# Three transformer blocks on one core: tokens in column order of the grid, and neighbourhood attention over 160 of 256 keys a tile

## The chip, the cores and the metric

The kernel is one program on one core of a Trainium2 chip, started once. The metric is device time in microseconds. Engines are named as in the profile: PE (matrix products, with its weight loads as PEld), DVE (vector), ACT (scalar), POOL (GpSimd), SP (the engine that issues nearly all transfers). All data are float32; "fp32r" marks operands that PE takes in one pass, and many products are made of three such passes over a high and a low part.

## The reference

256 tokens of 1024 features go through a first block of two layers and a second block.

- Layer 0: differential attention and latent attention over all 256 tokens (with rotary positions), output projection, residual times alpha, layer norm; then a mixture of experts (32 experts, two a token, grouped routing), residual times alpha, layer norm.
- Layer 1: neighbourhood attention, then the same tail with another mixture of experts.
- Second block: RMS norm, a gated linear recurrence with a causal convolution beside retention, output projection, and a gated feed-forward part with a causal convolution.

Neighbourhood attention sees the tokens as a grid of 4 rows and 64 columns, token = 64 row + column. It has 16 heads of 64. A query in column c attends to all 4 rows and to 16 columns, from clip(c - 8, 0, 48) on:

```
col_start = clip(cols - kw // 2, 0, GRID_W - kw)
s = einsum(q_row, k_win) * d**-0.5 + bias(head, row offset, column offset)
p = softmax(s over the 4 x 16 window);  o = p @ v_win
```

Layer 0 and the experts don't care in which order the tokens stand, as long as positions go with them. The second block does, since its convolutions, recurrence and retention run along the sequence.

## The kernel before

**Layout.** X holds the tokens as two tiles of 128 (partition = token in the tile). XT and MT hold features by tokens. The order is that of the sequence: tile 0 is grid rows 0 and 1, tile 1 is rows 2 and 3.

**Order of the work.** Each engine runs its own list of instructions, written out by hand; semaphores tie them together. On SP the loads stand in one queue in program order: each waits until the slot of the ring buffer that it fills is free, and everything behind waits with it. QKV weights (I_QKV), output weights (I_OO) and then the expert weights of layer 1 (load_experts) follow each other; the bias of the neighbourhood attention, one transfer of 128 x 16 x 384 numbers (source line 686 of the profile), stands behind the fourth QKV weight. It goes to G, in the arena. LNR holds the gain and bias of the coming norm; POOL loads it (norm_rows). The expert layer 0 keeps a copy of X there (XP).

**Neighbourhood attention** (functions `attention` on PE, ACT and DVE, a loop of POOL). For every head h and both query tiles t:
- PE makes the scores of 128 queries against all 256 keys (line 1037), for two heads at once since a head has 64 rows of the array, into banks 4 to 7.
- DVE adds the bias and takes the minimum in one instruction (2086); masked keys have a bias of -1e30. ACT takes the exponential with its sum (1623).
- DVE takes reciprocals (2093) and scales tile 1 (2095); POOL scales tile 0 (763).
- PE transposes the four 128 x 128 quarters (1049); ACT, for every fourth head DVE (2107), copies them out (1610).
- PE multiplies by the values, two matmuls of 256 columns a head (1062); ACT and DVE write the result as high and low part (1595, 2057).

PE works in pairs of heads: scores of pair i, transposes of pair i-2, values of pair i-3. PE's in-order list, the probability buffers PN (six) and PTN (four) set the order.

**After it.** The output projection (project_out_split, line 918) starts in the order of the pairs; POOL makes the low parts of the first two of its weight rows (767). DVE normalizes (mixed_norm), PE transposes X and makes the router's logits (1211), puts alpha times X into banks 0 to 3 with a diagonal matrix (`residual`, line 1216), and fills waits with matmuls that nobody reads (keep_clock, 1024). Banks 0 to 3 then gather the experts' outputs: for each pair of experts a matmul with the 0/1 matrix SWT (scatter, 1088; SWT is written by DVE, 2152) adds rows of outputs to their tokens. The gather (1074) uses SEL, its weighted copy is SELW. When 16 pairs are done, DVE normalizes from the banks into X.

**Loads of the expert layer.** Six weights of 2 MB a pair of experts. Ten places take them in turn; the first six of layer 1 wait for the end of QKV, for the end of attention (a_pv) or for the output projection, the rest for the pair before them in their place.

Of the kernel before, what the change touches and what calls it, by code (L numbers as in the profile page):

```python
# [15 lines left out]
P = 128  # L16
# [23 lines left out]
BIAS_ROWS = 6  # L40

# [23 lines left out]
def shape_constants():  # L65
# [3 lines left out]
    def rotation(theta, rot):  # L69
        inv = f(theta) ** (-np.arange(0, rot, 2, dtype=f) / f(rot))  # L70
        ang = np.arange(SEQ, dtype=f)[:, None] * inv[None].astype(f)
        both = np.stack([np.cos(ang), np.sin(ang)]).astype(f)
        return both.reshape(2, T, P, -1).transpose(2, 0, 1, 3).reshape(P, -1)
# [8 lines left out]
        rotation(500000.0, 2 * A_HALF),  # L82
        rotation(500000.0, B_ROPE),
# [30 lines left out]
def bass_two_blocks(nc, x, w_in, w_uq, w_ukv, w_o, w_qkv, na_bias, w_o2, ln_rows, rows, cols, w_route,  # L114
                    w_gate, w_up, w_down, w_in2, gates, w_out2, ffn_up, ffn_down, table, table2, out):
    with ExitStack() as ctx:
# [57 lines left out]

        ident, earlier = KT[:, K_ID:K_ID + P], KT[:, K_LT:K_LT + P]
# [35 lines left out]
        G = cut(4352, C_HEADS, BIAS_ROWS * GRID_W)  # L211
# [339 lines left out]
        def _(sp):  # L551
            sp.dma_start(KT[:, :], table).then_inc(x_loaded, 16)
            sp.dma_start(X[:, 0, :], x[0:P, :]).then_inc(x_loaded, 16)
            sp.dma_start(X[:, 1, :], x[P:SEQ, :]).then_inc(table2_loaded, 16)
# [113 lines left out]

            src, view = items[I_EIN[0]][0:2]
# [32 lines left out]
        def _(pool):  # L702
# [54 lines left out]
            pool.wait_ge(x_ready, 4)  # L757
            norm_rows(2)
            low_tiles(S_QKV, range(3 * TILES, 6 * TILES))
            for a in range(N_NA0, N_NA0 + C_HEADS):  # L760
                m = a % len(PN)
                pool.wait_ge(a_rec, a - N_NA0 + 1)
                nc.gpsimd.tensor_scalar(PN[m][:, 0, :], PN[m][:, 0, :], sm[:, m, 0:1], None,
                                        ALU.mult).then_inc(a_p0, 1)
            for c in range(ROWS_FIRST):
# [24 lines left out]
        def _(pe):  # L790
# [238 lines left out]
            def attention(a0, n, q, k, v, probs, probs_t, free):  # L1029

                for i in range(n // 2 + 3):
                    if i < n // 2:
                        for a in (a0 + 2 * i, a0 + 2 * i + 1):
                            if a - a0 >= 4:
                                pe.wait_ge(free, a - 3)
                            for t in range(T):
                                last = nc.tensor.matmul(bank[4 + a % 4][:, t * SEQ:(t + 1) * SEQ], q(a - a0, t), k(a - a0),
                                                        start=True, stop=True)
                            last.then_inc(a_score, 1)
                    if 0 <= i - 2 < n // 2:  # L1040
                        for a in (a0 + 2 * i - 4, a0 + 2 * i - 3):
# [5 lines left out]
                            for t in range(T):  # L1047
                                for kt in range(T):
                                    last = nc.tensor.transpose(
                                        bank[a % 2][:, kt * SEQ + t * P:kt * SEQ + (t + 1) * P],  # L1050
                                        probs[a % len(probs)][:, t, kt * P:(kt + 1) * P], ident)
                            last.then_inc(a_pt, 1)
                    if 0 <= i - 3 < n // 2:
# [6 lines left out]
                        for kt in range(T):  # L1060
                            for e in range(2):
                                last = nc.tensor.matmul(bank[2 + pair % 2][64 * e:64 * e + 64, 0:SEQ],
                                                        v(a - a0 + e, kt), probs_t[(a + e) % 4][:, kt, :],
                                                        start=(kt == 0), stop=(kt == T - 1))
# [134 lines left out]
            def moe_layer(l, name):  # L1199

                if l == 0:
                    pe.wait_ge(route_loaded, 16)
                for t in range(T):
                    if t:
                        keep_clock(6, 1)
                        transposes_by_token(name, X, x_ready, 4 * l, [t])
                        keep_clock(5, 1)
# [7 lines left out]
                    for half in range(2):  # L1215
                        nc.tensor.matmul(bank[2 * t + half][:, :], residual, X[:, t, 512 * half:512 * half + 512],
                                         start=True, stop=False, skip_group_check=True)

                keep_clock(5, 2)
# [1436 lines left out]
```

## Time and profile before

| | us |
|---|---|
| median of three timed runs (1503.03 to 1504.11) | 1503.18 |
| the profiled execution's own time | 1501.31 |
| its span, first to last instruction | 1499.4 |

| engine | busy us | share |
|---|---|---|
| PE | 1455.7 | 97% |
| DVE | 563.1 | 38% |
| ACT | 476.1 | 32% |
| POOL | 153.8 | 10% |

The stages by PE's chain: layer 0's attention to about 142 us, its experts to about 582, QKV of layer 1 from 591 to 660, neighbourhood attention from 661 to 689, projection and router to 726, experts to 1154, then the second block. Busy shares are averages over these. A time in the span is counted from its start; the timeline's rows begin with it, and the DMA share of a window is that of all 16 DMA engines. PE's clock was granted in full throughout.

### The profile page before, as it was taken

What the parts mean: (1) busy time and instruction counts of PE and PEld (TensorE: products, weight loads), DVE (VectorE), ACT (ScalarE), POOL (GpSimd) and SP (SyncE); (2) the same over time, 40 slices, a digit from 0 to 9 for tenths busy, and PEclk for the clock granted to TensorE, in tenths of its full rate; (3) what the DMA queues carried; (4) which work ended last, traced back from release to release, by engine and by line L of the source; (5) the groups of instructions that cost most, each with busy time, mean ns of one, the idle gap of its engine ahead of it and who ended that gap; (6) DMA issues with size and microseconds to landing.
All of it is one profiled execution on the core that took longest, in us unless ns stands there. A gap on an engine that the chain in (4) does not pass through costs nothing.

```text
span 1499.4 us, 19281 instructions
## 1 busy us (share of the span) xinstructions
PE 1455.7 (97%) x7750; PEld 881.1 (59%) x7750; DVE 563.1 (38%) x1161; ACT 476.1 (32%) x837; POOL 153.8 (10%) x124
## 2 busy tenths in 40 slices
PE   8989999999999998999999999999999999999997
PEld 7766444544544445977544545445444786888886
DVE  6675111121111113037311111111111488689965
ACT  4561111111111113456111111111111672687654
POOL 0211000000000002952100000000000710001200
PEclk9999999999999999999999999999999999999999
DMA  8657999999999999835999999999999946464410
GB/s 304 243 234 265 398 424 427 428 428 426 427 428 428 425 423 399 307 151 235 380 408 427 430 427 427 428 427 427 427 426 412 351 170 224 171 223 169 174 52 29
DMA packets 77669, 502.70 MB, mean 335 GB/s; under 512 B 4880, under 2 KB 6160, under 8 KB 50320
## 3 DMA queue, kind: packets, MB, share of 16 engines
q1 hardware_dynamic: 77008, 497.27, 81.4%
q0 software_dynamic: 576, 4.19, 0.7%
q8 instruction: 65, 1.06, 0.3%
q14 instruction: 20, 0.16, 0.0%
HBM read 500.40 MB, written 1.05 MB: 334 GB/s over the span
## 4 chain that ended last, share of the span: by engine, by line
PE 82%; DVE 7%; DMA 5%; ACT 2%; SPq 2%; issue 1%; POOL 0%; DVEq 0%; ACTq 0%
PE bank L1129 26%; PE bank L1170 13%; PE bank L990 9%; PE bank L1074 7%; DMA ring<-in_w_up 4%; PE bank L1456 4%; PE bank L1484 3%; PE bank L1088 3%; DVE w_low L2524 2%; SPq L649 2%; PE bank L899 2%; PE bank L1458 2%; PE bank L918 1%; PE bank L837 1%; DVE arena L2548 1%
## 5 line engine op out<-in xcount | busy, mean ns | idle before, releaser
L1129 PE MATMUL bank<-ring,arena 128*64 128x512 f32 x1280 | 280.6, 593 | 8.9 <-issue 5.5
L1129 PEld LDWEIGHTS bank<-ring,arena 128*64 128x64 f32 x1280 | 93.2, 137 | 191.3 <-issue 189.0
L1129 PE MATMUL bank<-arena 128*64 128x512 f32 x576 | 167.8, 592 | 0.0
L2143 DVE TENSOR_TENSOR arena<-arena,bank 128x512 f32<-128x512 f32 x32 | 22.0, 688 | 371.9 <-PE bank L1129 371.9
L1170 PE MATMUL bank<-ring,arena 128*64 128x512 f32 x640 | 141.7, 595 | 2.4 <-ACT arena L1638 2.4
L1456 PE MATMUL bank<-x_split,w_high 128*128 128x512 f32 (+1 forms) x408 | 136.3, 385 | 0.2 <-DVE x_split L1951 0.2
L1074 PEld LDWEIGHTS bank<-SEL,x_by_row 128*128 128x128 f32 x1024 | 116.7, 192 | 25.8 <-issue 24.3
L2157 DVE SCALAR_TENSOR_TENSOR y_low<-bank,ST,y_high 128x512 fp32r<-128x512 f32 x64 | 48.1, 751 | 202.4 <-ACT y_high L1642 202.4
L1074 PE MATMUL bank<-SEL,x_by_row 128*128 128x128 f32 x1024 | 122.8, 278 | 0.0
L1642 ACT ACTIVATE y_high<-bank,ST 128x512 fp32r<-128x512 f32 x64 | 44.0, 687 | 245.6 <-PE bank L1170 245.6
L1129 PEld LDWEIGHTS bank<-arena 128*64 128x64 f32 x576 | 54.8, 137 | 107.7 <-issue 107.7
L1458 PE MATMUL bank<-x_split,w_low 128*128 128x256 f32 (+1 forms) x408 | 111.5, 273 | 0.0
L2524 DVE TENSOR_TENSOR w_low<-ring,w_high 128x1024 fp32r<-128x1024 f32 x72 | 97.7, 1359 | 28.2 <-ACT w_high L1860 28.0
L712 POOL TENSOR_TENSOR qkv_low<-ring,qkv_high 128x1024 fp32r<-128x1024 f32 x24 | 58.2, 2441 | 457.8 <-DVE X L1997 449.8
L1635 ACT COPY arena<-bank 128x512 f32<-128x512 f32 x30 | 17.6, 586 | 253.6 <-PE bank L1074 253.6
L1170 PEld LDWEIGHTS bank<-ring,arena 128*64 128x64 f32 x640 | 45.9, 137 | 84.2 <-issue 84.2
L1456 PEld LDWEIGHTS bank<-x_split,w_high 128*128 128x128 f32 x408 | 76.3, 187 | 15.1 <-DVE x_split L1951 0.3
L1170 PE MATMUL bank<-arena 128*64 128x512 f32 x272 | 85.0, 595 | 0.0
L1129 PE MATMUL bank<-first_over_features,arena 128*64 128x512 f32 x192 | 84.4, 592 | 0.0
L1860 ACT CAST w_high<-ring 128x1024 fp32r<-128x1024 f32 x72 | 75.5, 1052 | 25.3 <-PE bank L1484 25.2
L1458 PEld LDWEIGHTS bank<-x_split,w_low 128*128 128x128 f32 x408 | 77.2, 189 | 0.0
L712 POOL TENSOR_TENSOR in_low<-ring,in_high 128x1024 fp32r<-128x1024 f32 x12 | 29.4, 2488 | 451.8 <-DVE X L1997 448.8
(369 smaller groups left out, 2222.7 us busy)
## 6 DMA issues: line engine op xcount, KB each, us to landing
ring<-in_w_gate SPq DMA_DIRECT2D x32, 2048.0 KB, 25.7
ring<-in_w_up SPq DMA_DIRECT2D x32, 2048.0 KB, 22.4
ring<-in_w_down SPq DMA_DIRECT2D x32, 2048.0 KB, 22.8
arena<-in_w_gate SPq DMA_DIRECT2D x18, 2048.0 KB, 22.5
arena<-in_w_down SPq DMA_DIRECT2D x16, 2048.0 KB, 24.1
arena<-in_w_up SPq DMA_DIRECT2D x14, 2048.0 KB, 16.5
ring<-in_ffn_up SPq DMA_DIRECT2D x12, 2048.0 KB, 7.9
ring<-in_w_in SPq DMA_DIRECT2D x8, 2048.0 KB, 15.0
```

Of the source, the lines that this page charges most:

```text
L712: nc.gpsimd.tensor_tensor(low, src, high, ALU.subtract).then_inc(w_lo, 1)
L990: last = nc.tensor.matmul(part_(bank[g % 2 * 2 + t]), a, b, start=(part_ is parts[0] and c == 0 and n == 0), stop=(part_ is parts[-1] and ...
L1074: last = nc.tensor.matmul(bank[6 + c // 4][:, c % 4 * P:(c % 4 + 1) * P], x_rows(t, c), SEL[:, t, :], start=(t == 0), stop=(t == T - 1))
L1088: last = nc.tensor.matmul(bank[2 * t + half][:, :], SWT[:, t, :], y[:, 512 * half:512 * half + 512], start=False, stop=False, skip_group_c ...
L1129: last = nc.tensor.matmul(bank[4 + m][64 * e:64 * e + 64, :], XG[:, c, 64 * e:64 * e + 64], w[e][:, c, :], start=(c == 0), stop=(c == C - 1))
L1170: last = nc.tensor.matmul(bank[6 + half][64 * e:64 * e + 64, :], HT[:, j, 64 * e:64 * e + 64], down_rows(e, j)[:, 512 * half:512 * half + ...
L1456: nc.tensor.matmul(bank[f % 4][:, :].rearrange("p (a b) -> p a b", a=2)[:, :, a:b], WHI[f % WBUF][:, c, :], XSPLIT[:, :, c, a:b], start=(a ...
L1458: last = nc.tensor.matmul(bank[f % 4][:, a:b], WLO[f % WBUF][:, c, :], XHI[:, c, a:b], start=False, stop=(b == SEQ and c == C - 1), skip_g ...
L1484: last = nc.tensor.matmul(bank[4 + 2 * t + half][:, :], a, w.rearrange("p a b -> p (a b)"), start=(c == 0 and n == 0), stop=(c == DOWN_T - ...
L1860: nc.scalar.copy(WHI[k % WBUF][:, :, :], src).then_inc(w_hi, 1)
L2157: v.scalar_tensor_tensor(YLO[:, cols_], bank[6 + half][:, :], slot_gate, YHI[:, cols_].bitcast(F32), ALU.mult, ALU.subtract).then_inc(s["y ...
L2524: v.tensor_tensor(WLO[k % WBUF][:, :, :], ffn_weights(k)[1], WHI[k % WBUF][:, :, :], ALU.subtract)\
```

## The change

1. x is loaded in column order: token = 4 column + row. Tile 0 is grid columns 0 to 31, tile 1 is 32 to 63. The rotary tables of layer 0 are laid out alike.
2. A query tile needs 40 columns, that is 160 keys: tile 0 keys 0 to 159, tile 1 keys 96 to 255. Scores, bias, exponential, scaling and copy work on 160 keys or queries. The gap of PN between the two parts is cleared by POOL.
3. The transposes become two whole ones, one of 64 rows and one of 32 rows a head. The values become three matmuls of 160, 96 and 64 columns.
4. The bias comes in 16 transfers (2 tiles, 2 sets of heads, 4 grid rows of the query), of 32 partitions each and pieces of 232 numbers. Its layout in DRAM is unchanged, so DVE reads it with the grid row as innermost index, 64 numbers apart. Heads 13 to 15 lie in LNR, so the load waits for the end of layer 0's last norm (x_ready 4), and norm_rows(2) moves behind the last bias reduction.
5. In layer 1 the residual and the scatter put rows back into sequence order: the diagonal matrix becomes four permuted ones (TO_ROWS, in SEL and SELW, written by POOL), eight matmuls instead of four, in the place of layer 1's keep_clock; SWT of layer 1 is written with permuted columns.

```diff
+KEYS = (GRID_W // 2 + NA_COLS // 2) * GRID_R          # 160
+KEYS_FROM = (0, SEQ - KEYS)                           # 0, 96
...
-            sp.dma_start(X[:, 0, :], x[0:P, :]).then_inc(x_loaded, 16)
-            sp.dma_start(X[:, 1, :], x[P:SEQ, :]).then_inc(table2_loaded, 16)
+            by_column = x.rearrange("(r c) d -> c r d", r=GRID_R)
+            for t, loaded in enumerate((x_loaded, table2_loaded)):
+                sp.dma_start(X[:, t, :], by_column[GRID_W // T * t:GRID_W // T * (t + 1)]).then_inc(loaded, 16)
...
+        def bias_of(h, t):
+            buffer, at = bias_block(h, t)
+            whole = buffer[:, at:at + GRID_R * GRID_W].rearrange("p (r j) -> p r j", j=GRID_W)
+            return whole[:, :, 0:KEYS // GRID_R].rearrange("p r j -> p j r")
...
+            def load_bias():
+                sp.wait_ge(x_ready, 4)
+                for t in range(T):
+                    for heads in (range(IN_ARENA), range(IN_ARENA, C_HEADS)):
+                        for r in range(GRID_R):
+                            begin = (2 - r // 2 * 2) * GRID_W + KEYS_FROM[t] // GRID_R
+                            first = r % 2 * GRID_W + GRID_W // T * t
+                            sp.dma_start(bias_blocks(t, heads)[r:P:GRID_R],
+                                         na_bias[first:first + GRID_W // T, heads[0]:heads[-1] + 1, begin:begin + BIAS_W])\
+                                .then_inc(bias_loaded, 16)
...
                 if i == I_QKV[3]:
-                    sp.dma_start(G[:, :, :], na_bias).then_inc(bias_loaded, 16)
+                    load_bias()
...  POOL
-            pool.wait_ge(x_ready, 4)
-            norm_rows(2)
             low_tiles(S_QKV, range(3 * TILES, 6 * TILES))
+            (two memsets and four copies: TO_ROWS; six memsets: the gap of each PN, the last two after pj_done 2 * G_OO)
             for a in range(N_NA0, N_NA0 + C_HEADS):
-                nc.gpsimd.tensor_scalar(PN[m][:, 0, :], PN[m][:, 0, :], sm[:, m, 0:1], None, ALU.mult)
+                nc.gpsimd.tensor_scalar(PN[m][:, 0, 0:KEYS], PN[m][:, 0, 0:KEYS], sm[:, m, 0:1], None, ALU.mult)
+            pool.wait_ge(a_nb, B_HEADS + C_HEADS)
+            norm_rows(2)
...  PE, attention
+                    edge, half = KEYS - P, P // 2
+                    return [(to[:, 0:P], p[:, 0, 0:P], ident),
+                            (to[:, SEQ + edge - half:SEQ + edge], p[half:P, 0, P:SEQ], ident[half:P, half:P]),
+                            (to[:, P:KEYS], p[0:edge, 1, 0:P], ident[0:edge, 0:edge]),
+                            (to[:, SEQ + edge:SEQ + KEYS], p[:, 1, P:SEQ], ident)]
...
+                        pieces = [(0, 0, SEQ, 0), (1, 0, SEQ, 0)] if not near else \
+                            [(0, 0, KEYS, 0), (1, KEYS, SEQ, KEYS_FROM[1]), (1, KEYS_FROM[1], KEYS, KEYS_FROM[1])]
...  PE, router of layer 1
-                    for half in range(2):
-                        nc.tensor.matmul(bank[2 * t + half][:, :], residual, X[:, t, 512 * half:512 * half + 512], ...)
-                keep_clock(5, 2)
+                nc.tensor.matmul(bank[2 * to + half][:, :], residual if same else TO_ROWS[t][:, to, :],
+                                 X[:, t, 512 * half:512 * half + 512], start=(same or t == 0), ...)
...  DVE, experts of layer 1
+                    v.tensor_scalar(SWT[:, :, :].rearrange("p t (r c) -> p (t r) c", c=GRID_W),
+                                    chosen.rearrange("p (c r) -> p r c", r=GRID_R), 0.0, None, ALU.is_gt)
```

## Rows read from the trace of the kernel before

**Rows 1.** Chain that ended last (start us, us, what), end of layer 1's experts.

```profile
1119.04 30.86 DMA ring<-in_w_up
```

**Rows 2.** Windows (stretch, length, busy us and instructions of each engine, PE clock, DMA share, GB/s).

```profile
640.00:660.00 20.00, 19.92 (x124) 17.68 (x122) 0.74 (x2) 6.17 (x7) 10.72 (x5) 1.00 0.00 0
...
700.00:706.00 6.00, 6.00 (x28) 4.97 (x27) 4.51 (x7) 0.30 (x1) 0.00 (x0) 1.00 0.20 85
...
850.00:900.00 50.00, 50.00 (x268) 23.72 (x266) 9.07 (x20) 8.86 (x12) 0.00 (x0) 1.00 1.01 427
```

**Rows 3.** Windows over the attention stage (PE, PEld, DVE, ACT, POOL in this order).

```profile
667.00:683.00 16.00, 15.98 (x124) 10.33 (x121) 14.37 (x70) 15.74 (x55) 11.47 (x11) 1.00 0.90 384
683.00:690.00 7.00, 6.10 (x44) 3.68 (x43) 4.11 (x13) 6.00 (x19) 5.69 (x6) 1.00 0.00 0
```

**Rows 4.** Timeline of PE (start us, us, engine line op, tile, shape, count).

```profile
660.79 3.91 PE L1037 MATMUL bank<-arena 64*128 64x256 f32 x24 [0.87 <-DVE arena L1962]
...
667.27 1.14 PE L1037 MATMUL bank<-arena 64*128 64x256 f32 x8
...
673.70 1.14 PE L1037 MATMUL bank<-arena 64*128 64x256 f32 x8
674.77 1.09 PE L1049 MATMUL bank<-KT,arena 128*128 128x128 f32 x8
675.79 1.08 PE L1062 MATMUL bank<-arena 128*64 128x256 f32 x8
676.80 1.14 PE L1037 MATMUL bank<-arena 64*128 64x256 f32 x8
```

**Rows 5.** The same timeline in narrow windows: rows begin at single records.

```profile
674.23 0.60 PE L1037 MATMUL bank<-arena 64*128 64x256 f32 x4
...
674.45 0.39 PE L1037 MATMUL bank<-arena 64*128 64x256 f32 x2
...
674.93 0.49 PE L1049 MATMUL bank<-KT,arena 128*128 128x128 f32 x3
...
675.04 0.49 PE L1049 MATMUL bank<-KT,arena 128*128 128x128 f32 x3
```

**Rows 6.** Timeline of PE, a narrow window in the router of layer 1.

```profile
719.63 0.61 PE L1211 MATMUL bank<-WR,XT 128*128 128x36 f32 x4
```

**Rows 7.** Groups by shape: shape, count, busy us, mean ns of one.

```profile
L1610 ACT COPY arena<-bank 128x512 f32<-128x512 f32 x12 | 7.0, 581 | 0.6 <-PE bank L1049 0.5
...
L1595 ACT CAST mixed_high<-bank 128x256 fp32r<-128x256 f32 x8 | 3.0, 380 | 0.7 <-PE bank L1062 0.7
...
L2107 DVE COPY arena<-bank 128x512 f32<-128x512 f32 x4 | 2.7, 686 | 1.5 <-PE bank L1049 1.5
...
L2071 DVE COPY MT<-bank 128x256 f32<-128x256 f32 x4 | 1.7, 423 | 2.1 <-PE bank L1062 2.1
```

**Rows 8.** Timelines of POOL, DVE and PE: filling and emptying of the stage.

```profile
664.39 2.23 POOL L763 TENSOR_SCALAR arena<-arena,ST 128x256 f32<-128x256 f32 x2 [11.75 <-DVE ST L2093]
...
687.32 0.69 DVE L2107 COPY arena<-bank 128x512 f32<-128x512 f32 x1 [1.53 <-PE bank L1049]
...
689.50 0.50 PE L918 MATMUL bank<-out_high,mixed_high 128*128 128x512 f32 x1
```

**Rows 9.** Timelines of SP, DVE, POOL and ACT in the QKV stage.

```profile
585.61 5.88 SPq L686 DMA_DIRECT2D arena<-in_na_bias  x1
...
590.41 1.28 DVE L1997 SCALAR_TENSOR_TENSOR X<-X,ST,arena 128x1024 f32<-128x1024 f32 x1
...
596.34 0.37 SPq L560 DMA_DIRECT2D ring<-in_w_qkv  x1
...
618.03 0.60 POOL L704 DMA_DIRECT2D LNR<-in_ln_rows  x1
...
628.95 1.05 ACT L1679 CAST qkv_high<-ring 128x1024 fp32r<-128x1024 f32 x1 [1.83 <-PE bank L990]
```

**Rows 10.** A window while QKV weights come in pieces of 2 KB.

```profile
585.00:590.00 5.00, 3.18 (x15) 1.80 (x14) 3.63 (x6) 3.98 (x6) 4.11 (x2) 1.00 1.05 384
```

More of the change, by code:

```diff
@@ L72, in rotation @@
         both = np.stack([np.cos(ang), np.sin(ang)]).astype(f)
+        if by_column:
+            both = both.reshape(2, GRID_R, GRID_W, -1).transpose(0, 2, 1, 3)
         return both.reshape(2, T, P, -1).transpose(2, 0, 1, 3).reshape(P, -1)
@@ L1027, in x_tile, with attention, transposes_of @@
                 return XT[:, c, t * P:(t + 1) * P]
-            def attention(a0, n, q, k, v, probs, probs_t, free):
+            def attention(a0, n, q, k, v, probs, probs_t, free, near=False):
+                def transposes_of(a):
+                    p, to = probs[a % len(probs)], bank[a % 2]
+                    if not near:
+                        return [(to[:, kt * SEQ + t * P:kt * SEQ + (t + 1) * P], p[:, t, kt * P:(kt + 1) * P], ident)
+                                for t in range(T) for kt in range(T)]
+                    edge, half = KEYS - P, P // 2
[3 more added lines that the diff above has]
+                            (to[:, SEQ + edge:SEQ + KEYS], p[:, 1, P:SEQ], ident)]
                 for i in range(n // 2 + 3):
@@ L1046, in attention @@
                                 pe.wait_ge(*probs_copied(a - 2))
[L1047 to L1051, printed above, removed]
+                            for to, p, one in transposes_of(a):
+                                last = nc.tensor.transpose(to, p, one)
                             last.then_inc(a_pt, 1)
@@ L1059, in attention @@
                             pe.wait_ge(a_o, pair - 1)
-                        for kt in range(T):
+                        pieces = [(0, 0, SEQ, 0), (1, 0, SEQ, 0)] if not near else \
+                            [(0, 0, KEYS, 0), (1, KEYS, SEQ, KEYS_FROM[1]), (1, KEYS_FROM[1], KEYS, KEYS_FROM[1])]
+                        for n_, (kt, begin, end, base) in enumerate(pieces):
                             for e in range(2):
-                                last = nc.tensor.matmul(bank[2 + pair % 2][64 * e:64 * e + 64, 0:SEQ],
-                                                        v(a - a0 + e, kt), probs_t[(a + e) % 4][:, kt, :],
-                                                        start=(kt == 0), stop=(kt == T - 1))
+                                last = nc.tensor.matmul(bank[2 + pair % 2][64 * e:64 * e + 64, begin:end],
+                                                        v(a - a0 + e, kt),
+                                                        probs_t[(a + e) % 4][:, kt, begin - base:end - base],
+                                                        start=(n_ == 0), stop=(n_ == len(pieces) - 1))
                         last.then_inc(a_pv, 1)
@@ L1202, in moe_layer, with residual_rows @@
                     pe.wait_ge(route_loaded, 16)
+                def residual_rows(t, to, half):
+                    same = l == 0
+                    nc.tensor.matmul(bank[2 * to + half][:, :], residual if same else TO_ROWS[t][:, to, :],
+                                     X[:, t, 512 * half:512 * half + 512],
+                                     start=(same or t == 0), stop=False, skip_group_check=True)
                 for t in range(T):
                     if t:
-                        keep_clock(6, 1)
+                        if l == 0:
+                            keep_clock(6, 1)
+                        else:
+                            residual_rows(0, 1, 0)
                         transposes_by_token(name, X, x_ready, 4 * l, [t])
-                        keep_clock(5, 1)
+                        if l == 0:
+                            keep_clock(5, 1)
+                        else:
+                            residual_rows(0, 1, 1)
                     for copied in (tr_act, tr_dve):
@@ L1214, in moe_layer @@
                         last.then_inc(logits_done, 1)
-                    for half in range(2):
-                        nc.tensor.matmul(bank[2 * t + half][:, :], residual, X[:, t, 512 * half:512 * half + 512],
-                                         start=True, stop=False, skip_group_check=True)
-                keep_clock(5, 2)
+                    for to in ([t] if l == 0 or t == 0 else range(T)):
+                        for half in range(2):
+                            residual_rows(t, to, half)
+                if l == 0:
+                    keep_clock(5, 2)
                 pe.wait_ge(r_one, l + 1)
@@ L2125, in first_tokens, with experts @@
                 v.tensor_copy(XG[:, 4:8, :], bank[7][:, :].rearrange("p (a b) -> p a b", b=P)).then_inc(s["xg_hi"], 1)
-            def experts(s, pair, n, g, next_pair=True):
+            def experts(l, s, pair, n, g, next_pair=True):
                 dve.wait_ge(s["sel_ready"], g + 1)
@@ L2233, in moe_layer @@
                         with dve.Fori(0, PAIRS) as p:
-                            experts(s, p, r * PAIRS + p, r * (PAIRS + 1) + p)
+                            experts(l, s, p, r * PAIRS + p, r * (PAIRS + 1) + p)
                     dve.wait_ge(over_free[l], ROUNDS_MORE * PAIRS + 1)
```

77 lines of the change are left out of this document (57 added, 20 removed).

## The prediction, made before the changed kernel had run

> **What bounds the kernel now.** I read the page first, then the chain of waits, then the one stage that the change rebuilds. The page says TensorE (PE) 97% busy, with the DMA engines full through both expert layers. The chain [rows 1] and the windows [rows 2] say where each holds: the neighbourhood attention and what follows it run at PE's pace, the expert layer runs at PE's pace until its last pairs, and there PE waits 30.9 us for a weight transfer [rows 1]. In that layer the transfers run at 427 GB/s without a gap [rows 2], so its end is fixed by when its stream of transfers gets going. That start hangs on PE's progress: the DMA engines have nothing to move from 683 to 689.6 and little from 700 to 706 [rows 2, 3], because the next loads wait for the end of attention and of the output projection. So whatever the attention stage gains or loses should arrive at the end one for one, and work that is moved inside the QKV stage should cost nothing as long as PE stays gapless there.
>
> The stage lasts from 660.79 (first scores) to 689.50 (output projection), 28.7 us [rows 4, 8]. Between 667 and 683 PE is busy 15.98 of 16 us, ACT 15.74, DVE 14.37, POOL 11.47 [rows 3]. The timeline of PE [rows 4] shows one period of two heads: scores 1.07, transposes 1.02, values 1.02, sum 3.11 us, and nothing between them. PE is the bound, ACT close behind (share of 16 us times 3.11: ACT 3.06, DVE 2.79, POOL 2.23 a period).
>
> **Inside PE's period.** Narrow windows of the same timeline [rows 5] show single starts. Score records run two at a time (heads on different row halves) and start 0.22 apart: 256 columns in two passes. Four such starts are 0.86; the phase takes 1.07, so 0.21 is not columns. Eight transposes start 0.11 apart: 0.87 of 1.02, 0.15 over. Value records, again two at a time and 256 columns, are 4 x 0.216 = 0.86 of 1.02, 0.15 over. These 0.15 to 0.21 come each time that the tile shape changes (64*128, 128*128, 128*64). Four router matmuls of only 36 columns take 0.61 together with an end of 0.28, so they start 0.11 apart [rows 6], and a record with a 128-column weight does not go below 0.11, however little it streams.
>
> The Trainium skill has this as a rule (TensorEngine Tiling (Array Packing), Key Properties): changing the tiling mode drains TensorE, changing only the tile does not. The trace agrees with the first half, with the 0.15 to 0.21 above. It speaks against this change, because the new transposes of one head go through 128, 64, 32 and 128 rows.
>
> **The change part by part.** Per period of two heads:
> - Scores: 160 of 256 columns, 0.216 x 160/256 = 0.135 a start, above the 0.11 floor. 4 x 0.135 + 0.21 = 0.75, was 1.07. Bounds 0.75 and 1.07.
> - Transposes: still four a head, two whole ones (128 rows), one of 64 rows, one of 32. In order that is T1, half, edge, T4, then the same again; T4 and the next T1 share a shape. Seven phases instead of one: 7 x 0.15 = 1.05, four whole transposes 4 x 0.11 = 0.44, four small ones between 0.03 (their 64 or 32 columns at the whole one's rate, less than the floor) and 0.11, say 0.07: 0.28. Sum 1.77, was 1.02. No row shows such a small transpose. Below: no drain at all, 0.44 + 0.12 + 0.15 = 0.71. Above: each small one like a score phase, 0.11 + 0.21 = 0.32, so 4 x 0.32 + 0.44 + 3 x 0.15 = 2.17, plus 0.45 if each needs two records (2.62). I take 1.77, nearest to the rows of transposes.
> - Values: 512 columns a head become 160 + 96 + 64 = 320, in six starts instead of four: 0.86 x 320/512 = 0.54, + 0.15 = 0.69. If the 0.11 floor held for 64-column weights too: 2 x 0.135 + 4 x 0.11 + 0.15 = 0.86. I take 0.70.
> - PE's period: 0.75 + 1.77 + 0.70 = 3.22, was 3.11. PE gets 0.11 slower while the others get faster.
> - ACT: from 512 to 256 columns a copy saves 0.20 [rows 7], 0.8 ns a column. Four exponentials of 96 columns less 0.31, one and a half copies of 192 less 0.23: 3.06 to about 2.5. DVE: 1.03 ns a column by its two copies; four bias reductions 0.40, copy 0.10, multiply up to 0.10: 2.79 to 2.2. POOL: 1.1 a head [rows 8] becomes between 0.68 (in proportion) and 1.08, say 0.75. So ACT, DVE and POOL have slack, and PE alone decides.
> - The bias operand of the reduction is now read four rows at a time, 256 bytes apart; before it was contiguous. No row shows such a read by DVE. The nearest row is the contiguous copy, 1.03 ns a column: at best nothing is added, at worst (my bound) every column costs that twice, 0.16 more each; a period of DVE is then 2.9, still below PE's, so it is paid only in the filling of the pipe, six reductions, 1.0 us. I put 0.3 into the sum.
>
> The Trainium skill (SBUF — State Buffer, the note on SBUF cachelines) says that each access that crosses to a new 16-byte line pays a penalty. By it the 0.3 would be 1.0; no row here shows such a read.
>
> **What lies where.** (a) Filling, 660.79 to 667.27: the first transpose waits for scores, three heads of reductions on DVE, an exponential, and POOL's multiply. Scores give 0.32, six reductions 0.60, POOL 0.33: 1.25 earlier; the transposes of the second head waited for POOL until 666.6 [rows 8] and now come right behind the first head's, which take 0.88 instead of 0.63 inside that wait. The next scores come 1.3 earlier. (b) Five full periods, 667.3 to 683.0: 5 x 0.11 = +0.5. (c) Emptying, 683.0 to 689.50, 6.5: after it transposes and values of two pairs, (1.77 + 0.70) + 1.77, then DVE's last copy and split before the last values (from 687.2 to 688.5, with the copy of [rows 8] in it, 1.28 less 0.20), then these values 0.70: 6.02, -0.5. Sum -1.3; with the bias read -1.0.
>
> **What is moved.** Loads: the bias was one transfer issued at 585.61. It becomes 16, behind a wait for the second tile's normalization (DVE, 590.41 + 1.28 = 591.7) [rows 9]. Queued behind that wait on SP are the fifth and sixth QKV weights (the fifth issued 596.34, when its slot was freed [rows 9]) and the two output weights. One issue takes 0.37 where the queue is not full: 16 x 0.4 = 6 us, so until 598 if nothing blocks; the fifth weight comes 2 us later, and ACT first reads it at 628.95. The bytes rise from 3.1 to 3.8 MB in pieces of 928 bytes. With 2 KB pieces the engines moved 384 GB/s [rows 10]: 10 us; at half that rate 20. Attention reads it at 662, and nothing is moved from 640 to 660 [rows 2]. Cost 0. Norm rows 2: POOL's issue of 0.60 at 618.03 [rows 9] goes, and comes behind POOL's last multiply (686.5), ahead of two low rows of the output weights that PE takes from 689.5; POOL gets there over 0.3 earlier. The transfer (1 MB, 2.4 us at 427 GB/s) falls beside 4 MB of expert weights at 690 to 700 and is read at 714 or later. Cost 0, at most 0.3. POOL's new clears and copies (14 small ones, at the row of 1.08 for 256 columns at most 15 us, nearest to 4) start at 652.6, where it was idle for 11.75 us [rows 8]; the last two wait for the end of the QKV products, just before 660. Up to 11 us they are hidden.
>
> Residual: eight matmuls in place of four and four fillers of the same shape; PE's time from 706 to 726 is unchanged, and the matrices for it lie in selection buffers that are next written after the ranking. The strided reading of the chosen slots (DVE, once a pair of experts) has DVE idle on both sides. The first load of x in another order has the same 4 KB pieces. Cost 0 each.
>
> **The sum.** The profiled execution took 1501.31 (span 1499.4 and 1.9 around it), the median of the three timed runs is 1503.18, 1.87 more. 1501.31 - 1.0 = 1500.3, on the median's scale 1502.2.
>
> **Rivals.** (1) No drain between the small transposes: T becomes 0.71, PE's period 2.16, and ACT's 2.5 is the bound. Five periods 5 x -0.61 = -3.05, emptying about -2.0 (2 x 0.71 + 0.70 + 1.08 + 0.70 = 3.9, and half a microsecond of POOL's 1.5 a pair shows), filling -1.8: -6.8, so 1496.4. For it: the array takes two row halves at once in the scores. Against: every change of shape in [rows 4] costs. (2) The small transposes are dearer than whole ones (each 0.32, T 2.17, and values 0.86): period 3.78, +0.67 x 5 = +3.3; emptying 2 x 2.17 + 0.86 + 1.08 + 0.86 = 7.14, +0.6; filling -0.9: +3.0, 1506.2, slower than before. There are 32 small transposes on the path (4 in each of 5 periods, 8 emptying, 4 filling), and from 0.03 us each above my price, or 0.22 + 0.03, the change loses. For it: score phases carry 0.21, not 0.15, and no row has a 32-row shape. (3) The bias comes late: only if it took over 70 us from 591.7; each us beyond is lost. (4) A gain is swallowed by the expert stream: loads of 660 to 682 end before attention does, against it; it would give 1503.2.
>
> **How the numbers follow.** What a measurement here can tell from no change is 0.2%, 3.0 us. Forecast (-3 to +3 around 1502.2, with rival 4) 0.58; rival 2 0.18, of which 0.12 lies over 3.0 and the rest under; rival 1 0.20; rival 3 0.04. Faster 0.21 (rival 1 and 0.01 of the forecast), slower 0.16, same 0.63. Range 1496.5 to 1506.0: from rival 1's time to just short of rival 2's; half of rival 1, a third of rival 2 and rival 3 lie outside, 0.2 together.
>
> **What would show it.** PE's period between two score phases: 3.2 (mine), 2.5 (rival 1), 3.8 (rival 2). Score phase 0.75, value phase 0.70, and in the transposes starts 0.2 apart around the 64- and 32-row ones instead of 0.11. First transpose near 664.5, fifth QKV weight issued near 598, no PE gap from 603 to 660, reductions of 0.32 (contiguous price, 0.42 less 0.10) or 0.48. If the stage after it or the end does not move with the end of attention, the one-for-one step is wrong.

## The result, and the profile after

The changed kernel takes 1516.55 us (median of 6, 1515.52 to 1518.18) against 1503.27 (6 runs, 1502.29 to 1504.49) of the kernel before: ratio 1.0086, 95% interval 1.0076 to 1.0097. That is slower by 13.3 us. The forecast was 1502.2, "no change" within 3.0, with a range from 1496.5 to 1506.0; the time lies outside it.

The profiled execution took 1517.61 (span 1515.8). The first thing to look at is the column that the prediction never used, PE's granted clock. Windows of the changed kernel (stretch, length, busy us and instructions of PE, PEld, DVE, ACT, POOL, then PE clock, DMA share, GB/s):

```profile
660.00:665.00 5.00, 3.79 (x28) 2.88 (x27) 1.77 (x8) 2.13 (x3) 0.52 (x2) 1.00 0.41 102
665.00:670.00 5.00, 3.94 (x19) 2.59 (x19) 4.69 (x28) 4.71 (x23) 2.70 (x4) 0.82 0.99 423
670.00:675.00 5.00, 5.00 (x30) 3.35 (x30) 2.72 (x13) 3.01 (x14) 1.96 (x3) 0.50 0.99 418
...
695.00:700.00 5.00, 5.00 (x30) 3.16 (x26) 1.34 (x5) 1.94 (x6) 3.12 (x4) 0.50 0.44 182
700.00:705.00 5.00, 5.00 (x33) 3.85 (x33) 1.85 (x5) 3.12 (x8) 1.44 (x2) 0.50 0.19 48
705.00:710.00 5.00, 5.00 (x22) 4.08 (x21) 5.00 (x9) 5.00 (x11) 0.00 (x0) 0.92 0.91 331
```

From about 668 until just behind the start of the output projection PE runs at 1.2 GHz instead of 2.4: in 5 us windows (1 - clock) x 5 / 0.5 adds up to 37.6 us at the lower level. From 670 on its busy share is 100% in them; a full PE row says nothing of the clock. In the kernel before, the clock was 1.00 in all of [rows 2, 3]. The timeline of PE shows what it does to the period, the answer to [rows 4]:

```profile
662.99 1.43 PE L1102 MATMUL bank<-arena 64*128 64x160 f32 x16 [0.88 <-DVE arena L2044]
664.75 1.49 PE L1102 MATMUL bank<-arena 64*128 64x160 f32 x8 [0.34 <-DVE ST L2169]
667.16 0.94 PE L1113 MATMUL bank<-KT,arena 128*128 128x128 f32 x4 [0.91 <-DVE arena L2181]
...
674.71 1.45 PE L1102 MATMUL bank<-arena 64*128 64x160 f32 x8
676.09 2.57 PE L1113 MATMUL bank<-KT,arena 128*128 128x128 f32 x8
678.58 1.34 PE L1126 MATMUL bank<-arena 128*64 128x160 f32 x12
679.85 1.45 PE L1102 MATMUL bank<-arena 64*128 64x160 f32 x8
...
703.88 0.80 PE L970 MATMUL bank<-out_high,mixed_high 128*128 128x512 f32 x1
```

By the starts, scores take 1.38, transposes 2.49, values 1.27: a period of 5.14 us, where 3.22 was forecast and 3.11 stood before. The stage, from the first scores to the output projection, lasts 703.88 - 662.99 = 40.9 us; before it was 28.7. That is 12.2 of the 13.3 us, and in a period PE waits for nobody. The others have slack, as forecast:

```profile
674.71:690.13 15.42, 15.42 (x86) 10.47 (x85) 8.17 (x40) 7.32 (x31) 4.75 (x6) 0.50 0.57 244
```

These are three periods: ACT 2.44 each (forecast 2.5), DVE 2.72 (2.2, at most 2.9), POOL 1.58 (1.5).

What lies around the stage hardly moved. In the profiled execution the first scores come 2.2 us later than before (662.99 against 660.79), nearly all of it since the first 15 us (first long matmul at 14.31, before at 12.15). The kernels below that are the same up to there begin their scores between 661.0 and 665.0, all later than the one profiled execution of the kernel before: part of the 2.2 us is scatter, and e9_x_plain looks at the rest. The first part of the output projection, from its first matmul to the transposes of X, takes 17.4 us instead of 16.8; its first 1.9 us still run at the lower level. From its second part to the experts nothing changed. Chain of waits of the kernel before, then of the changed one:

```profile
707.28 5.47 PE bank L918 x24
...
730.14 13.88 PE bank L1129 x64
```

```profile
722.26 5.47 PE bank L970 x24
...
745.11 13.88 PE bank L1194 x64
```

That is 22.86 us before and 22.85 now.

### The profile page after: what moved, and what is told of

Same layout as the page of the kernel before. It is cut to its first block, busy times and chain, and to the rows that moved or that the text cites. A ratio compares the mean times of both kernels' runs of the same rounds, so it can differ in the third digit from the quotient of the medians.

```text
span 1515.8 us, 19374 instructions
## 1 busy us (share of the span) xinstructions
PE 1473.6 (97%) x7782; PEld 892.5 (59%) x7782; DVE 561.2 (37%) x1161; ACT 472.7 (31%) x837; POOL 152.2 (10%) x136
## 4 chain that ended last, share of the span: by engine, by line
PE 89%; DMA 3%; DVE 3%; ACT 2%; issue 1%; SPq 1%; POOL 1%; DVEq 0%; ACTq 0%; POOLq 0%
PE bank L1194 28%; PE bank L1235 14%; PE bank L1042 9%; PE bank L1139 8%; PE bank L1535 6%; PE bank L1563 4%; PE bank L1153 3%; PE bank L1537 3%; DMA ring<-in_w_up 2%; PE bank L951 2%; PE bank L970 2%; PE bank L1113 1%; PE bank L889 1%; DMA ring<-in_w_in 1%; PE bank L1076 1%
## 5 line engine op out<-in xcount | busy, mean ns | idle before, releaser
L1139 PEld LDWEIGHTS bank<-SEL,x_by_row 128*128 128x128 f32 x1024 | 116.7, 192 | 25.8 <-issue 24.3
```

The lines of the kernel that those rows point to most:

```text
L1139: last = nc.tensor.matmul(bank[6 + c // 4][:, c % 4 * P:(c % 4 + 1) * P], x_rows(t, c), SEL[:, t, :], start=(t == 0), stop=(t == T - 1))
```

## The experiments

Each time stands beside runs of the kernel before on the same chip, and the ratio is to those. "Stage" is the distance from the first scores to the first matmul of the output projection, in the profiled execution alone. Its "filling" is the stretch up to the first full period, in which PE still waits for the other engines; the "emptying" is what follows the last scores. All start from the changed kernel. The clock of a stretch is known for the profiled execution; of the others only the mean over the whole run is known, and 3 us at the lower level change it by 0.001, within its scatter (0.995 to 1.000 for the kernel before).

| kernel | stage us | mean clock of its runs | median us (runs) | ratio to before, 95% |
|---|---|---|---|---|
| changed | 40.9 | 0.984 to 0.986 | 1516.55 (6) | 1.0086, 1.0076 to 1.0097 |
| e1_whole | 25.7 | 0.994 to 0.999 | 1501.95 (10) | 0.9991, 0.9979 to 1.0003 |
| e2_filling | 27.9 | 0.997 to 1.000 | 1502.98 (10) | 1.0003, 0.9993 to 1.0013 |
| e3_each | 38.1 | 0.984 to 0.996 | 1513.56 (4) | 1.0107, 1.0048 to 1.0165 |
| e4_scores | 37.7 | 0.991 to 0.996 | 1510.30 (5) | 1.0042, 1.0017 to 1.0067 |
| e5_scores_whole | 25.8 | 0.997 to 0.999 | 1499.89 (10) | 0.9984, 0.9975 to 0.9993 |
| e6_light | 39.1 | 0.985 to 1.000 | 1507.79 (10) | 1.0033, 1.0005 to 1.0062 |
| e7_both | 24.9 | 0.996 to 0.999 | 1499.49 (12) | 0.9979, 0.9970 to 0.9987 |
| e8_x | 24.9 | 0.997 to 0.999 | 1500.23 (11) | 0.9985, 0.9977 to 0.9994 |
| e9_x_plain | 24.9 | 0.996 to 0.999 | 1498.97 (9) | 0.9973, 0.9963 to 0.9983 |
| e10_bias | 23.6 | 0.996 to 0.999 | 1498.24 (7) | 0.9965, 0.9954 to 0.9977 |
| e11_first_scores | 25.2 | 0.997 to 0.999 | 1500.31 (11) | 0.9982, 0.9973 to 0.9991 |
| e12_order | 24.1 | 0.997 to 1.000 | 1499.61 (12) | 0.9973, 0.9964 to 0.9982 |
| e13_first_whole | 27.3 | 0.997 to 0.999 | 1501.04 (10) | 0.9988, 0.9979 to 0.9998 |
| e14_first_small | 28.4 | 0.993 to 0.996 | 1502.99 (10) | 1.0005, 0.9995 to 1.0015 |

**e1_whole**

```diff
-  (to[:, SEQ+edge-half:SEQ+edge], p[half:P, 0, P:SEQ], ident[half:P, half:P]), (to[:, P:KEYS], p[0:edge, 1, 0:P], ident[0:edge, 0:edge])
+  (to[:, P:SEQ], p[:, 1, 0:P], ident), (to[:, SEQ+edge-P:SEQ+edge], p[:, 0, P:SEQ], ident)
```

> The changed kernel with one edit: each head's four transposes of the neighbourhood attention are whole 128x128 ones again (the columns without keys are zeros already); scores of 160 and values of 320 columns stay. In the changed kernel PE's granted clock stood at 0.50 (1.2 GHz) from 670 to 705 us and the period of two heads was 5.14 us (scores 1.38, transposes 2.49, values 1.27). Theory S (the small transposes let the clock fall): clock 1.00 through the stage, PE's period 0.69 + 1.02 + 0.64 = 2.35, so DVE's 2.72 decides, stage near 25.5 us instead of 41, about 1501 us. Theory C (too few columns in scores and values): clock 0.50, period 1.38 + 2.04 + 1.27 = 4.7, about 1513. Theory F (the idle 2.1 us of the filling let it fall, and it stays down): as C, 1513.

In the profiled execution the clock falls all the same, but is back after 3.4 us instead of 37.6. Windows of e1_whole:

```profile
665.00:670.00 5.00, 3.96 (x21) 2.81 (x20) 4.14 (x24) 5.00 (x24) 3.08 (x4) 0.68 0.99 426
670.00:675.00 5.00, 5.00 (x58) 4.11 (x56) 4.66 (x25) 3.98 (x17) 2.43 (x4) 0.98 1.00 424
```

So neither theory alone: without any small transposes the clock still falls, but it is down for a far shorter time.

**e2_filling**

```diff
+ if near and i == 2: keep_clock(2, 1)      # ahead of the third scores
+ if near and i == 2: keep_clock(2, 2)      # ahead of the first transposes
```

> The changed kernel with three extra matmuls of 512 columns (0.43 us each at full clock) in the filling of the attention, one ahead of the third pair's scores and two ahead of the first transposes, where PE was idle for 0.34 and 0.91 us. Theory F: the clock stays 1.00, the period becomes 2.7 (DVE's), about 1501 us. Theories S and C: the clock still falls to 0.50 once the periods run, 5.14 a period, 1516 to 1517.

The clock stays up with the very same attention behind the filling. This is the trace in which the forecast can be read as it was meant. Windows, then timeline of e2_filling:

```profile
665.00:670.00 5.00, 5.00 (x27) 2.81 (x25) 4.26 (x25) 4.22 (x18) 3.05 (x5) 1.00 1.01 426
670.00:675.00 5.00, 5.00 (x51) 3.72 (x50) 4.06 (x21) 3.98 (x19) 2.63 (x4) 1.00 1.02 434
```

```profile
676.95 0.82 PE L1104 MATMUL bank<-arena 64*128 64x160 f32 x8
677.70 1.72 PE L1117 MATMUL bank<-KT,probs_over_x 128*128 128x128 f32 x8
679.35 0.77 PE L1130 MATMUL bank<-arena 128*64 128x160 f32 x12
680.05 0.82 PE L1104 MATMUL bank<-arena 64*128 64x160 f32 x8
```

Scores 0.75, transposes 1.65, values 0.70: 3.10 us. Theory F holds for the clock, but not its period of 2.7: the 2.57 was the slow period halved, and the shape changes don't halve.

**e3_each** (`keep_clock(2 + pair % 2, 1)` ahead of each pair's values) and **e4_scores** (`keys = slice(0, SEQ)` in PE's scores, DVE reads `ps[:, t, keys]`)

> The changed kernel with one extra matmul of 512 columns ahead of each pair's values. Theory C (too few columns a microsecond): the clock stays or comes back to 1.00, period 2.57 + 0.43 = 3.0, about 1503 us. Theory S: with the small transposes still there the clock stays 0.50, period 5.14 + 0.86 = 6.0, about 1523. Theory F: as S.

> The changed kernel with scores over all 256 keys on PE again (DVE still reads 160). Theory C: clock 1.00 again or for part of the stage, period 2.57 + 0.38 = 2.95, about 1503 us. Theories S and F: clock 0.50, period 5.14 + 0.76 = 5.9, about 1522.

In both the clock falls near 666 to 668 and comes back inside the stage: near 676.5 in e3_each, 687.7 in e4_scores. Either edit shortens the slow stretch and doesn't prevent it. One extra matmul of 512 columns was priced at 0.43; in e3_each it takes 0.95 (it is made of two records), so a period there is 3.96. Neither time was forecast by any of the theories. The executions of these two kernels scatter: three of e3_each took 1513.0 to 1513.9 and the fourth 1529.8 at a mean clock of 0.984, those of e4_scores 1504.1 to 1514.1. The length of the slow stretch in the one profiled execution is therefore not that of all.

**e5_scores_whole** (both edits, e1 and e4)

> The changed kernel with scores over all 256 keys on PE and whole 128x128 transposes (the shapes of the kernel before); values of 320 columns, and the narrow exponentials, reductions, copies and multiplies stay. With either alone the clock fell to 0.50 near 666 to 668 us. Theory P (what PE streams in the filling of the stage decides, narrow scores and small transposes both take from it): with both restored the clock stays 1.00, period 1.07 + 1.02 + 0.70 = 2.8, about 1501 us. Theory Q (something else of the change in the filling brings the fall, as the exponentials and copies that come at other times): the clock falls as well, and is back by about 672, about 1502 to 1503.

Theory P fits. Nothing is added, PE is idle about as long in the filling as in the kernel before, and the clock stays at 1.00 in the profiled execution; none of the ten means is low (0.997 to 0.999). First e5_scores_whole, then the kernel before, in the same two windows:

```profile
660.00:665.00 5.00, 4.11 (x27) 3.11 (x25) 2.31 (x10) 2.60 (x6) 0.52 (x2) 1.00 0.58 177
665.00:670.00 5.00, 3.94 (x27) 2.64 (x26) 4.70 (x27) 4.90 (x24) 3.08 (x4) 1.00 1.00 423
```

```profile
660.00:665.00 5.00, 3.89 (x24) 2.97 (x24) 3.56 (x18) 2.62 (x10) 0.61 (x1) 1.00 0.84 288
665.00:670.00 5.00, 3.90 (x28) 2.72 (x30) 4.55 (x27) 5.00 (x19) 4.33 (x5) 1.00 1.00 426
```

Over these 10 us PE is busy 7.79 before and 7.73 in the changed kernel: its busy share doesn't tell the one that keeps the clock from the one that loses it.

**e6_light** (only `keep_clock(2, 1)` ahead of the first transposes)

> The changed kernel with one extra matmul of 512 columns (0.95 us as measured) ahead of the first transposes, none ahead of the third scores. Theory G (any idle time filled is enough): the clock stays 1.00, the first transposes come 0.7 us earlier than with three extra matmuls, about 1502.3 us. Theory H (the fall hangs on the sum of the idle time, of which 1.2 us remain): the clock falls, about 1516, or in some executions only.

Neither theory's single time: it is a coin toss, as the last words of theory H allowed: five executions took 1500.2 to 1502.5 at a mean clock of 0.997 to 1.000, five 1513.1 to 1516.8 at 0.985 to 0.987. The profiled one is of the second kind; its clock fell at 670, after five microseconds in which PE was busy 4.83. The median of all ten stands for neither group. A kernel can be measured at 1501 and at 1515 with nothing changed.

**e13_first_whole** (small transposes behind the first four heads only) and **e14_first_small** (in the first four heads only), both with 256-key scores for the first six heads

```diff
+ if a - a0 < 4:      # e14: a - a0 >= 4
+     return (the four whole transposes of e1)
```

> The changed kernel with scores over 256 keys for the first six heads, whole transposes for the first four, and the small transposes and 160 keys for all heads behind them; no extra matmul. Theory P (the filling of the stage decides; the running periods with small transposes hold a clock that is up, as in e2_filling): clock 1.00, periods of 3.10, stage 25.2 + 5 x 0.5 + 0.6 = 28.3 us, about 1503 us. Theory R (the first running periods count as well): the clock falls to 0.50 near 670 as in e6_light and stays down to the output projection, stage 37 to 39, 1512 to 1516, in all or some executions.

> The reverse: scores over 256 keys for the first six heads, the small transposes for the first four heads alone, whole ones behind them; no extra matmul. Theory P: the clock falls to 0.50 near 667 and is back by 671 (as in e1_whole), stage 26 to 27, 1501 to 1502.5 us. Theory R: it stays 1.00 or is down more briefly, stage 25.8, about 1500.7.

Theory P is right on whether the clock falls. Windows of e13_first_whole, then of e14_first_small:

```profile
665.00:670.00 5.00, 3.67 (x29) 2.37 (x29) 4.82 (x27) 5.00 (x24) 3.50 (x5) 1.00 0.99 423
670.00:675.00 5.00, 5.00 (x51) 3.71 (x51) 4.33 (x23) 4.03 (x18) 2.75 (x4) 1.00 1.03 434
```

```profile
665.00:670.00 5.00, 4.25 (x24) 2.52 (x22) 4.51 (x27) 4.93 (x23) 3.08 (x4) 0.90 1.00 429
670.00:675.00 5.00, 5.00 (x29) 3.58 (x30) 2.58 (x14) 2.08 (x9) 1.58 (x2) 0.50 1.02 431
675.00:680.00 5.00, 5.00 (x56) 4.33 (x54) 4.48 (x25) 4.22 (x18) 2.52 (x4) 0.92 0.98 419
```

The timeline of e14_first_small shows where:

```profile
666.55 0.94 PE L1118 MATMUL bank<-KT,arena 128*128 128x128 f32 x4 [0.59 <-DVE arena L2186]
667.66 0.94 PE L1118 MATMUL bank<-KT,arena 128*128 128x128 f32 x4 [0.17 <-issue]
...
669.49 2.57 PE L1118 MATMUL bank<-KT,probs_over_x 128*128 128x128 f32 x8
```

The clock falls near 669, when only the first two heads' transposes have run, four small ones among them; the next two heads' already run at the lower level. Twenty-four small transposes behind the filling, in periods of 3.10, don't bring a fall. All ten executions of e14_first_small have a mean clock of 0.993 to 0.996, all ten of e13_first_whole 0.997 to 0.999, as the kernel before beside them (0.996 to 1.000). PE is busier in the filling that loses the clock (8.36 of 10 us, the last one at half clock) than in the one that keeps it (7.77). What theory P got wrong is how long: e14_first_small's clock was to be back by 671 and is back near 675.8, which makes its stage 28.4 instead of 26 to 27.

**e7_both** (e2 and e1 together) and **e11_first_scores** (whole transposes, 256-key scores for six heads, nothing added)

> The changed kernel with three extra matmuls in the filling of the attention and whole transposes. If the small transposes cost what the trace at full clock shows (1.65 for two heads against 1.02), PE's period falls from 3.10 to 2.47 and DVE's 2.6 to 2.7 decides: 5 x 0.45 + 1.0 in the emptying = 3.2 us less than with the small ones, about 1499.8 us. If another engine bounds the stage already, no gain: 1503.

> The changed kernel with whole transposes, scores over all 256 keys for the first six heads alone and over 160 for the others, and no extra matmul. Theory P (what PE streams in the filling decides): the clock stays 1.00 as in e5_scores_whole, and the periods are those of e7_both, 2.6 instead of 2.8: 1499.0 us. Rival (the scores of the periods that follow count as well): the clock falls to 0.50 for some microseconds in some or all executions, as in e1_whole, 1501 to 1502.

e7_both does what it was meant to: 3.0 us of stage less than e2_filling, and 3.2 us (0.21%) faster than the kernel before. The starts of its scores at 673.50, 676.11 and 678.67 give a period of 2.6, as forecast. e11_first_scores keeps the clock without any added work and has the same periods; 0.9982 is not told apart from 0.9979.

**e8_x** and **e9_x_plain**, both on e7_both

```diff
- sp.dma_start(X[:, t, :], by_column[32 * t:32 * (t + 1)])                 # twice
+ e8: sp (tile 0), act (tile 1): dma_start(X[r:P:4, t, :], x[64 * r + 32 * t:64 * r + 32 * t + 32])   # r = 0..3
+ e9: sp.dma_start(X[:, t, :], x[P * t:P * (t + 1), :])
```

> As e7_both, and x is loaded in eight transfers, each of 32 rows that lie behind one another in memory (four on SP's queue for the first tile, four on ACT's for the second). Theory X (the 2.2 us by which the first long matmul comes later than before are the slower transfer of rows picked 64 apart): most of the 2.2 comes back, 1497.6 us. Rival (the issues cost as much as they save, or the delay is not in this transfer): 1499.8 or later.

> As e7_both (three extra matmuls in the filling, whole transposes), with x loaded as in the kernel before: each tile 128 rows that lie behind one another. Left out: the order of the tokens, so everything behind works on tokens in the wrong places. Theory X (the transfer of rows picked 64 apart costs): the second tile is there near 5 instead of 8.1 us and the first long matmul starts 1 to 2 us earlier; the ratio to before falls from 0.9979 by 0.001. Rival (the other 1 us is scatter between executions): first long matmul at 13.3 as before, ratio 0.998.

Chains of waits of e7_both, e8_x and e9_x_plain, first microseconds:

```profile
1.89 6.20 DMA X<-in_x
...
13.46 41.65 PE bank L1042 x192
```

```profile
3.06 4.96 DMA X<-in_x
...
15.38 41.63 PE bank L1041 x192
```

```profile
1.64 5.97 DMA X<-in_x
...
12.52 41.88 PE bank L1041 x192
```

With rows that lie behind one another the long matmuls start 0.9 us earlier, and the time is 0.9 us less by the ratios, but the intervals overlap: about 1 us of the miss can be the load of x, and it is not shown to be. The second tile lands at 7.6 instead of 8.1, not near 5 as theory X had it, and the long matmuls still start 0.4 us later than in the kernel before. Cutting it in eight was a miss: SP's queue has two more issues of 0.6 us, and the first weight behind them is issued at 3.69 instead of 2.52.

**e10_bias** (`buffer[:, at:at + KEYS]` as bias) and **e12_order** (scores and result `"p (j r) -> p r j"`, the bias in its own runs of 40), both on e7_both

> As e7_both, with the bias of the reduction read as 160 values that lie behind one another. Left out: the right bias, each value comes from another place of the same buffer. If the strided read is what keeps the reduction at 0.42 us for 160 columns (before: 0.42 for 256), it falls to 0.32, DVE's period from 2.6 to 2.2, PE's 2.47 decides, 5 x 0.13 + 0.6 in the filling: about 1 us less than e7_both. Rival (0.42 has another cause, as the operand in the score bank): it stays 0.42 and so does the time.

> As e7_both, and the reduction walks its three operands grid row by grid row (four runs of 40): the bias is then read in runs, while the scores and the result are stepped over four apart. Nothing is left out. With the bias in runs and all else too (e10_bias) the reduction took 0.32 us, with the bias stepped 0.42. Theory: it is any stepped operand that costs, so it stays at 0.42 or rises with two of them stepped (up to 0.52, then DVE's period is 3.0 and the time 1501 to 1502). Rival: only the operand in the state buffer that is read pays; then 0.32 and the time of e10_bias, ratio 0.9965.

The two reductions of a head in the timeline of DVE (start, then length of the record), e7_both, e10_bias, e12_order:

```profile
677.41 0.42 DVE L2173 CUSTOM_DVE_ANT_1 arena<-bank,arena 128x160 f32<-128x160 f32 x1
...
677.76 0.43 DVE L2173 CUSTOM_DVE_ANT_1 arena<-bank,arena 128x160 f32<-128x160 f32 x1
```

```profile
676.55 0.31 DVE L2172 CUSTOM_DVE_ANT_0 arena<-bank,arena 128x160 f32<-128x160 f32 x1
...
676.79 0.32 DVE L2172 CUSTOM_DVE_ANT_0 arena<-bank,arena 128x160 f32<-128x160 f32 x1
```

```profile
676.92 0.45 DVE L2173 CUSTOM_DVE_ANT_1 arena<-bank,arena 128x160 f32<-128x160 f32 x1
...
677.22 0.45 DVE L2173 CUSTOM_DVE_ANT_1 arena<-bank,arena 128x160 f32<-128x160 f32 x1
```

With the bias stepped a record lasts 0.42 to 0.43, as much for 160 columns as the contiguous one for 256; with scores and result stepped 0.45, with none 0.32. But the records overlap, and what one costs in a period is the distance to the next start: 0.35 with the bias stepped by 64 elements, 0.24 with nothing stepped and 0.30 with scores and result stepped by 4 (the kernel before: 0.34 for 256 columns). In e10_bias DVE's period falls and PE's own 2.48 decides (scores at 673.16, 675.64, 678.11), 1.3 us of stage; its time is 0.14% below e7_both's, with intervals that overlap. e12_order runs at 2.48 too: its records are longer, but its starts are 0.05 closer, four times a period. Its expectation priced the records: by them its theory is right (0.45), by the starts the price lies between theory and rival.

## Why the prediction was wrong

**The step that failed** is the one beneath the whole sum: every term of "The change part by part" takes its start distances (0.216, 0.135, 0.11) from rows at 2.4 GHz, and the stage ran at 1.2. Its period became 5.14 us instead of 3.22, the stage 40.9 us instead of 27.7. The clock was in the windows that the prediction read [rows 2, 3], at 1.00, and no rival asked what could take it away. The runs put in its place: the filling of the stage, with idle pieces of 0.88, 0.34 and 0.91 us around narrow scores and small transposes, loses the clock. Small transposes of the first heads are enough for it (e14), and so are scores of 160 keys (e1); filling the idle pieces (e2) or the old shapes in the filling (e5, e11, e13) keeps it. Once down, it stayed down as long as narrow scores and small transposes followed, 37.6 us, and returned after 3.4 us with whole ones. PE's busy share doesn't sort these cases; which matmuls stand in the filling does. Why it does, these runs don't show: the cause is shown as far as which edits lose the clock and which keep it, and the step from there to a rule is open.

The Trainium skill (TensorE: Matmul & The Clock Gate, Part 1) has the slow clock as the default, which activity releases. The trace of the changed kernel doesn't agree as that stands: PE worked without a gap from 669.6 to 705.7, and the granted clock was 0.50 all that time.

**Point by point**, with the clock up (e2_filling), the forecast's own steps:
- Period 3.22, measured 3.10: scores 0.75 (0.75), values 0.70 (0.70), transposes 1.65 (1.77). Rival 2 (3.78) and rival 1 (2.5) are both refuted at full clock. The seven phases are right in kind. From the two clocks the shape changes can be estimated: if a time is one part that halves at the doubled clock and one that doesn't, the latter is 2 x 1.65 - 2.49 = 0.81 for the transposes, or 0.12 for each of seven (0.15 forecast). The same for scores is 2 x 0.75 - 1.38 = 0.12, for values 0.13. So the trace agrees with the rule of the Trainium skill that the prediction cited (TensorEngine Tiling (Array Packing), Key Properties).
- Stage -1.0, measured 27.9 - 28.7 = -0.8, with three extra matmuls in it; e13_first_whole, with no extra ones, -1.4. That they lie so near is partly luck. From the starts in e2_filling the five periods give -0.25 (forecast +0.5) and the emptying -0.7 (-0.5). The filling is 0.1 longer with its three extra matmuls; forecast was 1.0 shorter, the bias read included. The changed kernel, still at full clock there, has its first transposes 4.17 us behind its first scores, before 4.78: 0.6 earlier, where the prediction's 1.25 less 0.3 was expected. Its term for the six reductions is what is missing: 0.60 less 0.3, while the first six take 2.08 us by their starts in both kernels.
- Bias read: 0.3 in the sum, from a bound of 0.16 more a reduction. Measured 0.10 more by the records and 0.11 by the starts (e7_both against e10_bias), so 0.6 for six. It also costs in the periods once PE is faster than DVE (e10_bias). The Trainium skill's note on lines of 16 bytes (SBUF — State Buffer) has the sign right; it names no price, so the 1.0 that the prediction gives beside it is the prediction's own bound.
- The bias load on SP was priced at 6 us; the timeline of SP in the changed kernel has 16.4 us for the 16 issues (0.65 each in the third group of four, 1.7 in the first), and the fifth QKV weight is issued at 610.8, not 598:

```profile
594.44 6.96 SPq L703 DMA_DIRECT2D arena<-in_na_bias  x4
601.44 3.66 SPq L703 DMA_DIRECT2D LNR<-in_na_bias  x4
605.15 2.61 SPq L703 DMA_DIRECT2D arena<-in_na_bias  x4
607.80 2.96 SPq L703 DMA_DIRECT2D LNR<-in_na_bias  x4
610.81 1.41 SPq L586 DMA_DIRECT2D ring<-in_w_qkv  x2
```

  The step's cost of 0 held: PE had no wait from 600 to 662. Its cover of 33 us was wide enough for an error of 13, about 3 of it the later end of the norm (594.4, forecast 591.7).
- "The first load of x has the same 4 KB pieces. Cost 0": perhaps 1 us (e9), within the scatter. It was priced by the size of the pieces alone.
- POOL's clears and copies lie in its idle time, the last before 657.7 and two at 662; the residual, the scatter and the norm rows cost nothing, 22.85 against 22.86 us.
- "Whatever the stage gains arrives one for one": right within about 1.6 us. Change of the stage, and (ratio - 1) x 1503: the changed kernel +12.2 and +12.9 (0.6 of it in the projection), e5 -2.9 and -2.4, e7 -3.8 and -3.2, e10 -5.2 and -5.3, e13 -1.4 and -1.8, e14 -0.3 and +0.8, e2 -0.8 and +0.5, e1 -3.0 and -1.4. Where executions fall into groups (e3, e4, e6), one profile can't be set against a median.

## What to carry to other kernels

Price a stage's filling for PE's clock, not only for time: where a change makes the matmuls narrower or smaller while PE waits for the other engines, ask what keeps the clock, and make "half the clock until the shapes change" a rival with its price (here 13 us on a stage of 28). To mend it, put extra or full-size matmuls into the filling alone; the running periods needed nothing here (e2, e13). With one extra matmul instead of three the kernel has two times (e6), so look at several executions. Save columns on the engines behind PE first: e5_scores_whole keeps PE's old scores and transposes and gains 2.4 us. On PE itself, both the narrow scores and the new tile shapes cost the clock here.

## What was not expected of the hardware

- PE at 1.2 GHz and 100% busy for over 35 us, against a return after 3.4 us with whole transposes, 10.3 us with an extra matmul in each period and 20.5 us with wider scores (one profiled execution each).
- The same program in two groups of times 14 us apart (e6_light).
- A reduction on DVE over 160 columns, by the distance of its starts: 0.24 us with nothing stepped, 0.30 with two operands stepped by 4 elements, 0.35 with one stepped by 64. The length of its record (0.32, 0.45, 0.42) gives another order.
- Issues of transfers in 928-byte pieces hold SP's queue for 0.65 to 1.7 us each, against 0.4 for plain ones.
